# Softmax division moved to ScalarE, and 32 modulation rows turned from GpSimd/ScalarE work into VectorE dot products

## What is computed

```
mod = split(silu(c) @ ada_w[i] + ada_b[i], 6)          # shift, scale, gate, shift, scale, gate
h = rmsnorm(x, g[0]) * (1 + mod[1]) + mod[0];   y = mixer(h)
x = x + mod[2] * rmsnorm(y, g[1])
h = rmsnorm(x, g[2]) * (1 + mod[4]) + mod[3]
x = x + mod[5] * rmsnorm(mlp(h), g[3])
p = softmax(q k / sqrt(128));   o = p v                # in the attention
```

## Times and profile before

| what | us |
|---|---|
| median of 3 runs | 1598.87 (1598.76 to 1599.36) |
| the profiled execution, as timed | 1602.27 |
| its span in the trace, first to last instruction | 1600.5 |
| TensorE busy in the span | 1393.8 (87%) |
| VectorE busy | 966.8 (60%) |
| ScalarE busy | 639.8 (40%) |
| GpSimd busy | 272.4 (17%) |

### The profile page before, as it was taken

One profiled execution on the slowest core, in us unless ns is written; L12 is line 12 of the kernel. 1 busy time (PEld: TensorE's weight loads), 2 busy tenths in 40 slices (PEclk: granted clock), 3 DMA queues, 4 the chain that ended last, 5 costly groups with the idle time before them and its releaser, 6 DMA issues. The chain is left out here.

```text
span 1600.5 us, 17418 instructions
## 1 busy us (share of the span) xinstructions
PE 1393.8 (87%) x6186; PEld 1094.0 (68%) x6186; DVE 966.8 (60%) x1223; ACT 639.8 (40%) x960; POOL 272.4 (17%) x164
## 2 busy tenths in 40 slices
PE   6997878777949999999977967978895999999995
PEld 1455656776827888888854756867772888888884
DVE  5785986988475445454567688788628333333344
ACT  2234433777335343443424433334323434343440
POOL 0503333665420000000151000000052000000022
PEclk9998999999979999999997979989996999999998
DMA  8443112343315545464521112121220232322221
GB/s 321 149 171 132 53 51 95 129 136 115 121 67 171 183 150 193 136 204 131 175 74 62 70 66 79 53 79 53 79 92 13 93 106 92 103 93 92 95 89 52
DMA packets 46093, 176.78 MB, mean 110 GB/s; under 512 B 5367, under 2 KB 5623, under 8 KB 42520
## 3 DMA queue, kind: packets, MB, share of 16 engines
q1 hardware_dynamic: 44312, 165.61, 30.5%
q0 software_dynamic: 1728, 10.49, 1.9%
HBM read 165.59 MB, written 10.49 MB: 110 GB/s over the span
## 5 line engine op out<-in xcount | busy, mean ns | idle before, releaser
L1375 PE MATMUL bank<-hhi,whi 128*128 128x512 f32 x864 | 348.5, 403 | 34.7 <-DVE hlo L946 22.3
L1376 PE MATMUL bank<-hlo,whi 128*128 128x512 f32 x864 | 340.5, 394 | 0.0
L1377 PE MATMUL bank<-hhi,wlo 128*128 128x512 f32 x864 | 340.2, 394 | 0.0
L933 DVE TENSOR_TENSOR wlo<-raw,whi 128x1024 fp32r<-128x1024 f32 x168 | 216.8, 1293 | 67.8 <-ACT whi L614 67.3
L1375 PE MATMUL bank<-ghi,whi 128*128 128x512 f32 x576 | 224.8, 390 | 4.6 <-DVE glo L1314 4.6
L1377 PE MATMUL bank<-ghi,wlo 128*128 128x512 f32 x576 | 224.8, 390 | 0.0
L1376 PE MATMUL bank<-glo,whi 128*128 128x512 f32 x576 | 224.6, 390 | 0.0
L1375 PEld LDWEIGHTS bank<-hhi,whi 128*128 128x128 f32 x864 | 164.9, 191 | 83.5 <-issue 32.6
L614 ACT ACTIVATE whi<-raw 128x1024 fp32r<-128x1024 f32 x180 | 188.7, 1051 | 6.6 <-DMA raw<-in_wpack 5.7
L1376 PEld LDWEIGHTS bank<-hlo,whi 128*128 128x128 f32 x864 | 165.4, 191 | 35.1 <-issue 2.5
L1377 PEld LDWEIGHTS bank<-hhi,wlo 128*128 128x128 f32 x864 | 164.8, 191 | 35.2
(11 more groups left out here) (243 smaller groups left out, 2260.4 us busy)
## 6 DMA issues: line engine op xcount, KB each, us to landing
raw<-in_wpack SPq DMA_DIRECT2D x180, 512.0 KB, 3.3
araw<-in_apack SPq DMA_DIRECT2D x40, 512.0 KB, 3.3
amore<-in_apack SPq DMA_DIRECT2D x24, 512.0 KB, 3.3
ablk<-in_ahead SPq DMA_DIRECT2D x8, 1024.0 KB, 9.2
spectra<-scratch SPq DMA_DIRECT2D x8, 1024.0 KB, 4.2
scratch<-in_apack SPq DMA_DIRECT2D x16, 512.0 KB, 3.3
araw<-spectra POOLq DMA_DIRECT2D x8, 1024.0 KB, 5.1
fs<-in_decay SPq DMA_DIRECT2D x8, 256.0 KB, 3.7
```

Of the source, the lines that this page charges most:

```text
L933: TT(wlo[:, s, :], raw[:, r, :], f(whi[:, s, :]), ALU.subtract).then_inc(lo_done, 1)
L1375: mm(o, lh, rh, start=first, stop=False)
L1376: mm(o, lh, rl, start=False, stop=False)
L1377: return mm(o, ll, rh, start=False, stop=last)
```

## The change

ScalarE divides the probabilities, as a copy with a scale per partition, at the head of its iteration n; VectorE keeps the reciprocal. The rows are counted anew, r = 0 to 79 for rows 16 to 95. All are made by VectorE's multiply-and-sum: r = 0 to 7 in the attention, at the end of the iterations n = 3, 7, ... 31; r = 8 to 23 in the output projection, two behind the preparation of each unit; r = 24 to 79 in the MLP, 16 behind the units of each of three quarters and 8 in the last. GpSimd's products and ScalarE's sums go. SP loads the rows in that order between the units. `modulation(1)` moves behind the output projection's loop and no longer needs rows 40 to 47, whose gain is made in `modulation(2)`. VectorE's code of the first quarter becomes part of its loop, and the last quarter is written out.

```diff
 # ScalarE, attention
             for n in range(NQ + 5):
+                m = n - 2
+                if 0 <= m < NQ:
+                    act.wait_ge(rinv_done, m + 1)
+                    A(PROB[m % 2], PROB[m % 2], ACT.Copy, scale=rinv[:, m % 2:m % 2 + 1]).then_inc(p_done, 1)
                 if n >= 6 and n % 2 == 0:
...
-                a = n - 4
-                if 0 <= a < 32:
-                    act.wait_ge(amul_done, a + 1)
-                    slot = arow_slot(16, a % ADA_RING)
-                    A(slot, slot, ACT.Copy, accum_out=mods[:, 16 + a:17 + a]).then_inc(asum_done, 1)
 # GpSimd, attention
-            pool.wait_ge(crow_done, 1)
-            for a in range(16, 48):
-                pool.wait_ge(arow_in[a % ADA_RING], 16 * (a // ADA_RING - 3))
-                slot = arow_slot(a, a % ADA_RING)
-                nc.gpsimd.tensor_tensor(slot, slot, crow, ALU.mult).then_inc(amul_done, 1)
 # VectorE
+            def ada_row(k, loads, dst, early=False):
+
+                dve.wait_ge(arow_in[k], 16 * loads)
+                slot = arow_slot(k, early)
+                nc.vector.tensor_tensor_reduce(slot, slot, crow if early else crow1[:, :], 1.0, 0.0, ALU.mult, ALU.add,
+                                               dst).then_inc(arow_done, 1)
+
             for n in range(NQ + 5):
                 m = n - 2
                 if 0 <= m < NQ:
                     dve.wait_ge(exp_done, m + 1)
                     if m >= 2:
                         dve.wait_ge(p_done, m - 1)
-                    own(nc.vector.reciprocal(rinv[:, m % 2:m % 2 + 1], rsum[:, m % 2:m % 2 + 1]))
-                    TS(PROB[m % 2], PROB[m % 2], rinv[:, m % 2:m % 2 + 1], None, ALU.mult).then_inc(p_done, 1)
+                    nc.vector.reciprocal(rinv[:, m % 2:m % 2 + 1], rsum[:, m % 2:m % 2 + 1]).then_inc(rinv_done, 1)
...
                 if n >= 6 and n % 2 == 0:
                     o_lo((n - 6) // 2)
-            modulation(1)
+                if n < NQ and n % 4 == 3:
+                    r = n // 4
+                    if r == 0:
+                        dve.wait_ge(crow_done, 1)
+                    ada_row(r % ADA_RING, r // ADA_RING + 1, mods[:, 16 + r:17 + r], True)
...
             dve.wait_ge(lo_done, U_OUT0 + AHEAD)
+            dve.wait_ge(crow_done, 2)
             for j in range(OUT_UNITS):
                 prep(U_OUT0 + j + AHEAD, (j + AHEAD) % 4, (j + AHEAD) % 2)
+                for r in range(ADA_ATT + 2 * j, ADA_ATT + 2 * j + 2):
+                    ada_row(r % ADA_RING, r // ADA_RING + 1, mods[:, 16 + r:17 + r])
...
+            modulation(1)
             boundary(0)
-            dve.wait_ge(crow_done, 2)
-            quarter(0, 0)
-            with dve.Fori(1, QUARTERS) as q:
+            with dve.Fori(0, QUARTERS - 1) as q:
                 quarter(0, q)
+            quarter(0, QUARTERS - 1, last=True)
 # SP
+            for r in range(ADA_ATT):
+                load_row(r, r % ADA_RING, r - ADA_RING + 1 if r >= ADA_RING else None, True)
+            for r in range(ADA_ATT, ADA_ATT + ADA_RING):
+                if r == ADA_ATT + 2:
+                    sp.wait_ge(olo_done, NQ // 2)
+                load_row(r, r % ADA_RING, r - ADA_RING + 1)
+            for j in range(OUT_UNITS):
+                u = U_OUT0 + 5 + j
+                load_unit(u, u % 2)
+                for r in range(2 * j + ADA_ATT + ADA_RING, 2 * j + ADA_ATT + ADA_RING + 2):
+                    load_row(r, r % ADA_RING, r - ADA_RING + 1)
```

More of the change, by code:

```diff
@@ L65 @@
 AHEAD = 3
-ADA_START = [0, 16, 48, 96]
+ADA_START = [0, 16, 40]
 ADA_RING = 4
 ADA_HEAD = 8
-ADA_QUARTER = 48 // QUARTERS
+ADA_OUT = 24
+ADA_ATT = 8
+ADA_QUARTER = 16
+ADA_ROWS = 80
 C_G, C_AB, C_QG, C_KG = 0, 64, 160, 161
@@ L194, in build @@
         crow_done = sem("crow_done")
-        amul_done = sem("amul_done")
-        asum_done = sem("asum_done")
-        asum1_done = sem("asum1_done")
+        arow_done = sem("arow_done")
         bias_done = sem("bias_done")
@@ L341, in build, with arow_slot @@
         crow = S[:, 6:8, :].rearrange("p a b -> p (a b)")
-        def arow_slot(a, k):
+        def arow_slot(k, early=False):
             if k < 2:
                 return araw[:, k, :]
-            if a < 48:
+            if early:
                 return S[:, 4 + 2 * k:6 + 2 * k, :].rearrange("p a b -> p (a b)")
@@ L460, in _, with load_row, load_quarter @@
             sp.wait_ge(job_lo, len(JOBS))
-            for a in range(16, 48):
[L462 to L471, removed]
+            def load_row(r, k, used=None, early=False):
+                if used is not None:
+                    sp.wait_ge(arow_done, used)
+                sp.dma_start(arow_slot(k, early), apack[r]).then_inc(arow_in[k], 16)
+            for r in range(ADA_ATT):
[9 more added lines that the diff above has]
+                    load_row(r, r % ADA_RING, r - ADA_RING + 1)
+            def load_quarter(q, rows):
                 for s in range(16):
                     load_unit(U_MLP0 + 5 + 16 * q + s, (s + 1) % 2)
[L475 to L478, removed]
+                    if s < rows:
+                        r = ADA_OUT + ADA_QUARTER * q + s
+                        load_row(r + ADA_RING, s % ADA_RING, r + 1)
             with sp.Fori(0, QUARTERS - 1) as q:
-                load_quarter(q)
-            load_quarter(QUARTERS - 1, last=True)
+                load_quarter(q, ADA_QUARTER)
+            load_quarter(QUARTERS - 1, ADA_ROWS - ADA_RING - ADA_OUT - (QUARTERS - 1) * ADA_QUARTER)
             load_units(U_HY + 5, UNITS)
@@ L553, in y_squares @@
                         else:
-                            pool.wait_ge(asum_done, 32)
+                            pool.wait_ge(arow_done, ADA_ATT)
                         pool.dma_start(S[:, 8:10, :], tables[:, 2 * third:2 * third + 2, :]).then_inc(table2_in, 16)
@@ L582, in _ @@
             x_pairs(1)
-            pool.wait_ge(asum1_done, 48)
+            pool.wait_ge(arow_done, ADA_ROWS)
             def load_spectrum(m):
@@ L958, in modulation @@
             def modulation(b):
-                a, a1 = ADA_START[b], ADA_START[b + 1]
-                l = a // 48
-                bias = col[:, C_AB + a:C_AB + a1]
+                l = b // 2
                 if b == 0:
@@ L966, in modulation, with gated @@
                     for v in range(2):
-                        own(TT(mods[:, 96 * v:96 * v + 16], acols[:, v, :], bias, ALU.add))
+                        own(TT(mods[:, 96 * v:96 * v + 16], acols[:, v, :], col[:, C_AB:C_AB + 16], ALU.add))
                 elif b == 1:
-                    dve.wait_ge(asum_done, 32)
-                    own(TT(mods[:, a:a1], mods[:, a:a1], bias, ALU.add))
+                    dve.wait_ge(arow_done, ADA_OUT)
+                    own(TT(mods[:, 16:40], mods[:, 16:40], col[:, C_AB + 16:C_AB + 40], ALU.add))
                 def scaled(dst, m, g, v=0):
-                    return STT(dst, mods[:, 96 * v + 48 * l + 8 * m:96 * v + 48 * l + 8 * m + 8], 1.0, col[:, C_G + 8 * g:C_G + 8 * g + 8], ALU.add, ALU.mult)
-                def gated(dst, m, g):
-                    return TT(dst, mods[:, 48 * l + 8 * m:48 * l + 8 * m + 8], col[:, C_G + 8 * g:C_G + 8 * g + 8], ALU.mult)
+                    at = 96 * v + 48 * l + 8 * m
+                    return STT(dst, mods[:, at:at + 8], 1.0, col[:, C_G + 8 * g:C_G + 8 * g + 8], ALU.add, ALU.mult)
+                def gated(ll, m, n):
+                    at = 48 * ll + 8 * m
+                    g = C_G + 8 * (4 * ll + n)
+                    return TT(gain[:, ll, n, :], mods[:, at:at + 8], col[:, g:g + 8], ALU.mult)
                 if b == 0:
                     own(scaled(gainc[:, :], 1, 0, 1))
[L980 to L987, removed]
+                    last = scaled(gain[:, 0, 0, :], 1, 0)
+                elif b == 1:
+                    own(gated(0, 2, 1))
+                    last = scaled(gain[:, 0, 2, :], 4, 2)
+                else:
+                    own(gated(0, 5, 3))
+                    own(scaled(gain[:, 1, 0, :], 1, 4))
+                    own(gated(1, 2, 1))
+                    own(scaled(gain[:, 1, 2, :], 4, 6))
+                    last = gated(1, 5, 3)
                 last.then_inc(mod_done, 1)
@@ L1182, in quarter @@
                 c0 = l * 32 + 8 * q
+                rows = 0 if l else ADA_QUARTER if not last else ADA_ROWS - ADA_OUT - (QUARTERS - 1) * ADA_QUARTER
                 def modulate(s):
[L1186 to L1190, removed]
+                    if s < rows:
+                        ada_row(s % ADA_RING, 7 + 4 * q + s // ADA_RING, asum[:, s:s + 1])
                 for j in range(8):
@@ L1198, in quarter @@
                     u = u0 + 8 + j
-                    if not last or u + AHEAD < UNITS:
+                    if not last or not isinstance(u, int) or u + AHEAD < UNITS:
                         prep(u + AHEAD, (j + AHEAD) % 4, (j + AHEAD) % 2)
@@ L1207, in quarter @@
                     modulate(8 + j)
[L1208 to L1212, removed]
```

(8 more changed lines are left out.)

## The result

The changed kernel takes 1617.26 us, the median of 4 runs (1616.63 to 1619.21), against 1598.82 (1596.08 to 1599.36): 1.0112 times the time before, 95% interval 1.0092 to 1.0132, so it is slower by 1.1%. The forecast was 1617.0.

The account below looks back on a forecast made before the run. TensorE bounds projection and MLP; in the attention, near VectorE's limit, the engines' order counts. 15.4 us for the attention plus 2.7 for the clock, 18.1, gives 1620.4 profiled, 3.4 lower as median: 1617.0 against 1598.87, range 1608 to 1626.

Parts of the forecast that it names:

- The attention with its start: Attention: longer steps and later first phi add 15.4 us, TensorE's lower clock 2.7, together 18.1.
- the boundary: Behind the projection: VectorE ends near 444, reciprocal starts at 446.84, so 2.7 us of cover and no growth.
- The round: Attention, phi, plo, nmax, hlo or row, reciprocal, division, phi: steps of 4.01, 3.98, 5.12 us; 75%.
- Its last two: Attention's final steps: n = 32 without nmax, 3.15 us; n = 33 set by the transposes, 2.90.
- The division: ScalarE in the attention: the scaled copy lets the next instruction go after 0.85 us, bounds 0.81 to 0.91.
- The start: Attention: the first division and the wait for the second move the first phi 1.75 us later.
- The clock: TensorE in the attention: four of eight gaps behind row steps cost 0.67 us each, 2.7, bounds 0 and 5.4.
- The projection: Output projection: two 1.14 us dot products a unit stay hidden, VectorE needing 10.5 us against TensorE's 10.9 per two units.
- The rival's 17 us: Output projection: dot products double beside GpSimd and VectorE bounds it, 17 us more, 1634; 5%.
- The MLP: MLP: a unit takes 5.44 us with a row or without, so 8 more rows cost nothing.
- The rival with the faster outcome: Attention: the round does not bind, the ring through AB sets the pace; 31 steps 107.1 us, 1589.2; 7%.
- F + 2.9: Attention: 2.9 us after phi's start F, when TensorE's transposes are done; a division ending earlier would not bind.

Follow-up runs that it names:

- experiment 8: Changed kernel with TensorE computing scores twice more for n = 4, 8, ... and once more for n = 2, 6, ...: 1617.40 us, ratio 1.0107.
- Experiment 1: Changed kernel with VectorE's reciprocal made earlier, for block n-1 between plo and nmax of iteration n: 1588.64 us, ratio 0.9921 to the kernel before.
- experiment 2: Changed kernel with the division back on VectorE behind the reciprocal, rows left where the change put them: 1589.69 us, ratio 0.9925.
- 3: Kernel before with only the division moved to ScalarE, rows staying with GpSimd and ScalarE: 1607.45 us, ratio 1.0041.
- Experiment 6: Changed kernel with a third VectorE dot product per unit in the output projection, output unchanged: 1626.14 us, ratio 1.0173.
- experiment 5: Changed kernel with TensorE computing the scores of n = 4, 8, ... 28 twice, to shorten its gap behind row steps: 1617.65 us, ratio 1.0105.

## Why the prediction was right, and where it was not

**The total** came out within 0.3 us of the median, and that is in part luck. The attention with its start grew by 17.7 us where 18.1 were forecast, and the boundary by 1.6 where 0 was; that makes 19.3, and the medians differ by 18.4. The difference lies in the stretches that vary from execution to execution.

**The round** held as worked out. Steps of 4.01, 3.98 and 5.12 were forecast; 3.99 to 4.01, 3.92 (where the clock stayed up, experiment 8) and 5.07 came. Most of the 0.06 of the odd ones is `hhi`, which lets `phi` go 0.26 us after its start (297.58 to 297.84) and not 0.30. Experiment 1 shows that this order is the cause and not ScalarE's division as such. In experiment 2 the reciprocal stands as late as in the changed kernel, but no `phi` stands behind the division, and the long steps are gone too. The forecast's first 29 steps make 124.3 us without the clock's term, 1.0 more than the 123.35 of experiment 8. Its last two, 3.15 and 2.90, came as 3.55 and 3.39: behind a gap of 4.23 us the six transposes took 1.51 us (403.47) instead of 0.85 and let `phi` go late, and the values behind them held up the last transposes. The sum took the second of these steps as set by the transposes alone.

**The division** takes 0.936 us and gives way after 0.84 to 0.85 (296.74 to 297.58, 301.00 to 301.84); 0.85 was taken. **The start** costs 1.75, as forecast.

**The clock** was put at 2.7 us, four gaps of eight at 0.67. Experiment 8 gives 2.4. The transposes and the step behind one of the gaps, to be held against the earlier trace rows:

```profile
312.12 0.84 PE L1549 MATMUL bank<-consts,scratch 128*128 128x128 f32 x6
...
317.20 1.31 PE L1549 MATMUL bank<-consts,scratch 128*128 128x128 f32 x6 [3.17 <-DVE plo L1160]
...
322.66 0.82 PE L1549 MATMUL bank<-consts,scratch 128*128 128x128 f32 x6
```

The transposes take 1.31 us behind a gap of 3.17, and the next ones in line start 5.46 later. The steps that should take 3.92 took 4.60, 4.28, 4.32, 4.29, 4.16, 4.10 and 4.05. So it was seven gaps at 0.34 on the mean, with more of them and each cheaper than in the forecast (four at 0.67): two errors that cancelled. The rule of the Trainium skill in TensorE: Matmul & The Clock Gate (section HAM oscillation), that gaps bring the clock down again and again, held better than my count of half; its price by that count, 5.4, did not come (2.4).

**The projection** is the step that failed. The prediction said that dot products keep to 1.22 us beside GpSimd, with the 24 of the earlier trace rows as the reason, and gave VectorE 2.7 us of cover at the boundary. The dot products of the changed kernel (ns min/median/max; first those of the projection and the MLP on `araw`, then four of the attention):

```profile
L1145 DVE CUSTOM_DVE_ANT_0 araw<-araw,crow x36: 1212/1218/2300, 417.1 to 791.0; 128x1024 f32<-128x1024 f32 x36
...
L1145 DVE CUSTOM_DVE_ANT_0 araw<-araw,scratch x4: 1216/1216/1216, 278.3 to 364.7; 128x1024 f32<-128x1024 f32 x4
```

Up to 2300 ns where GpSimd works, 1216 in the attention, where it doesn't. In the earlier trace rows the chance of the order had kept them apart or let GpSimd give way. The kernel before shows the second, first on VectorE and then on GpSimd:

```profile
789.75 1.22 DVE L1189 CUSTOM_DVE_ANT_0 araw<-araw,crow 128x1024 f32<-128x1024 f32 x1
...
790.89 2.05 DVE L933 TENSOR_TENSOR wlo<-raw,whi 128x1024 fp32r<-128x1024 f32 x1
```

```profile
789.97 1.89 POOL L561 TENSOR_TENSOR scratch<-scratch 128x512 f32<-128x512 f32 x1 [303.59 <-DVE scratch L1206]
...
811.73 1.04 POOL L561 TENSOR_TENSOR scratch<-scratch 128x512 f32<-128x512 f32 x1 [1.32 <-DVE scratch L1206]
```

The square that started behind the dot product took 1.89 us instead of 1.04, and the split (`wlo`) that started during it 2.05 instead of 1.22. The projection of the changed kernel has both orders within 6 us, again VectorE first:

```profile
431.12 2.09 DVE L1145 CUSTOM_DVE_ANT_0 araw<-araw,crow 128x1024 f32<-128x1024 f32 x1
...
436.51 1.22 DVE L1145 CUSTOM_DVE_ANT_0 amore<-amore,crow 128x1024 f32<-128x1024 f32 x1
```

```profile
431.09 1.03 POOL L563 TENSOR_TENSOR scratch<-scratch 128x512 f32<-128x512 f32 x1 [1.24 <-ACT scratch L774]
...
436.58 2.04 POOL L563 TENSOR_TENSOR scratch<-scratch 128x512 f32<-128x512 f32 x1 [2.23 <-ACT scratch L774]
```

In these pairs the instruction that starts first keeps its length and the other one pays. From 427.7 to 461.1 us twelve of VectorE's instructions took 2.05 to 2.31 us, six of them dot products. The Trainium skill's GPSIMD Engine Reference (section Specifications) says that VectorE instructions with two SBUF inputs contend with GpSimd; the trace agrees, and I had let one group of rows outweigh it. At the boundary, VectorE and ScalarE:

```profile
457.91 1.21 DVE L934 TENSOR_TENSOR wlo<-raw,whi 128x1024 fp32r<-128x1024 f32 x1
459.05 2.05 DVE L1145 CUSTOM_DVE_ANT_0 amore<-amore,crow 128x1024 f32<-128x1024 f32 x1
...
461.03 1.22 DVE L1145 CUSTOM_DVE_ANT_0 amore<-amore,crow 128x1024 f32<-128x1024 f32 x1
...
462.29 0.18 DVE L969 TENSOR_TENSOR mods<-mods,cols 128x24 f32<-128x24 f32 x1
...
462.91 3.35 DVE L938 RECIPROCAL scratch<-scratch 128x512 f32<-128x512 f32 x1
```

```profile
457.60 0.60 ACT L774 ACTIVATE scratch<-bank 128x512 f32<-128x512 f32 x1 [3.89 <-PE bank L1393]
...
461.24 0.69 ACT L785 ACTIVATE scratch<-bank,eps 128x512 f32<-128x512 f32 x1 [1.74 <-PE bank L1577]
```

ScalarE's root (461.24) comes 3.64 us behind the last chunk instead of 2.99, as GpSimd's square is slowed (1.68 us instead of 1.04; 0 to 0.5 was allowed, 0 taken), and ends at 461.93; VectorE is in its rows and `modulation(1)` until 462.9. VectorE ends last, so the 1.6 us are its delay, and the 0.65 of the root lie under it. The forecast had VectorE done 0.9 us behind the start of the last chunk (444 against 443.13) with 2.7 to spare; it was done 5.3 behind it (462.9 against 457.60). The traces of experiments 1 and 2 have 5.30 there too, that of 3, without rows in the projection, 3.71. No run takes GpSimd's squares away; that they are what lengthens the dot products rests on the times shown. The rival's 17 us did not come, because its 2 x (2.3 + 4.6) + 1.3 takes all instructions at twice their length, and only those are that lie beside GpSimd's. Experiment 6 shows that the cover was used up: a third dot product in each unit costs 7.5 us there.

**The MLP** keeps to 5.44 us a unit, as said.

The rival with the faster outcome named its own condition, a division that ends before F + 2.9. Experiment 1 meets it, and its 107.1 us for 31 steps compare with 105.05.

Open: why the stretches ahead of the attention and behind the boundary differ by 3.2 and 1.4 us between the executions, and what exactly of TensorE's idle time brings the clock down. Experiments 5 and 8 show no more than one arrangement of gaps in which it fell and one in which it didn't.

## What to carry to other kernels

Moving work to an idle engine can pay only if it doesn't lengthen the chain that goes round from block to block; before such a move, write down that chain with the place of each instruction in its engine's order, for the order decides what the result waits behind. Even in the right order the division on ScalarE (1588.64) gained nothing that can be told over the one on VectorE (1589.69). A short instruction that another engine waits for goes ahead of long ones that nobody needs yet. Totals by engine told nothing here: VectorE got 38 us freer in the attention and the kernel 18 us slower.

## What the runs showed of the hardware

- A VectorE dot product of 128x1024 floats with both inputs in SBUF took 1.21 to 2.31 us beside GpSimd's work in SBUF, 1.216 without. The division by a scalar per partition (128x768) took 0.62 us without GpSimd (all 32 of experiment 2, and the first one of the kernel before, at 275.14, ahead of GpSimd's first product); over the 32 of the kernel before it took 0.62 to 2.85, 1.44 on the mean.
- The granted clock fell behind a gap of 2.90 us and all six of 3.17 in the changed kernel, and behind five of six of about 2.11 in experiment 5. With no gap over 1.1 us it was 1.00 for the 117 us from 280 to 397 in experiment 8, and for these 85 us in experiment 1:

```profile
280.00:365.00 85.00, 72.00 (x524) 66.27 (x524) 60.33 (x128) 70.90 (x115) 0.00 (x0) 1.00 0.12 38
```
